# Seven-product MLP pairs: two of the three passes joined into one 512-column product, and the first blocks' weights split by ScalarE and VectorE

## The chip, the cores and the metric

The kernel is one program on one core of a Trainium2 chip. The metric is the device time of one execution in microseconds (us). Before the change the median of three runs is 2317.03 us (2315.73 to 2317.9).

## The reference, cut to what matters

The program runs three transformer-like layers in fp32 on one sequence of T = 512 tokens with D = 1024 features: an RWKV layer, a forgetting-attention layer and a hybrid layer. Each ends in the same kind of MLP, and the change touches these three MLPs alone:

```
def sq_relu_mlp(h, w_in, w_out):
    return jnp.square(jax.nn.relu(h @ w_in)) @ w_out     # h: 512 x 1024, w_in: 1024 x 4096, w_out: 4096 x 1024
# x = x + sq_relu_mlp(rmsnorm(x, gain), w_in, w_out)
```

## The kernel before

**Three passes.** Every fp32 product W x is made from fp32r parts: W is split into whi (rounded) and wlo (the rest), x into hi and lo, and TensorE adds whi*hi + whi*lo + wlo*hi into one PSUM bank. `three` (L732 to L734) does so with 512 columns (tokens) for each of the three. Tokens lie along the columns, features along the 128 partitions.

**Weights.** They come as a stream of blocks of 128 x 1024 (512 KB). SyncE loads block b into `raw[b % 4]`, once block b - 4 is split. As a rule GpSimd makes `whi` (L508, or L582 in the MLP loops; counter `hi_ready`) and then `wlo` (L521; counter `split_ready`), each into slot b % 2, which is free when TensorE has finished block b - 2 (counter `blk`). TensorE waits on `split_ready` ahead of every block.

**An MLP** (`mlp(m, ...)` on TensorE, ScalarE and VectorE, m = 0, 1, 2) has 64 blocks. Blocks 0 to 7 of it are eight tiles of `h @ w_in` made in the plain way (`up`), blocks 8 to 11 are the first part of `@ w_out` (`down`, banks 4 to 7), and then a loop of three turns runs twice per turn: two *pairs* of up tiles (`pair_up`), then four blocks of `down`. The hidden tiles that a `down` reads are those of one group earlier. Blocks 60 to 63 are the last `down`.

**A pair** makes two up tiles (256 rows of the product) from two blocks of weights with seven products instead of eight, by a Strassen-Winograd scheme. Weights are combined into seven forms of 512 columns: VectorE makes four sums `SW` (`form_sum`, L2526), ScalarE rounds each form to `FH` (`form_high`, L1853), GpSimd makes the rest `FL` (`form_lows`, L569). The input is combined once for an MLP into seven forms p = 0 to 6 of 256 columns: `BF` the sum, `BH` its rounded part (ScalarE, L1840), `BL` the rest (VectorE, `x_form_low`, L2512). TensorE runs product p over four k with three passes of 256 columns each (L1184 to L1186), into banks 0, 1, 2, 3 and again 0, 2, 3. Counters: `prod` after p = 0 to 4, `blk` after p = 5 and 6.

**Out of the banks.** For a pair: ScalarE copies bank 0 after p = 0 to `tmpB` (`snapshot`, L1860); VectorE makes V = bank 1 - tmpB (`difference`, L2535), VT = bank 2 + V (L2542), a quarter of the result from bank 3 and VT (`fourth_quarter`, L2550), and later the second (L2555) and third quarter (L2560); ScalarE makes the first (L1865). Relu, square and rounding follow on ScalarE, and the low parts `hidL` on VectorE (`hidden_low`, L2566). The counters `chain` (VectorE) and `snap` (ScalarE) tell TensorE when a bank may be written again.

**Order.** All engines run hand-written orders, each in order. In a half turn VectorE (`group_of_pairs`) does: sums 0 and 1 for the second pair, difference, VT, fourth quarter of the first pair, sums 2 and 3 for the second pair, second and third quarter, then the difference of the second pair, `hidden_low`, VT, `hidden_low`, fourth quarter and the rest. GpSimd does the seven `FL` of the first pair, the seven of the second, and then whi and wlo of the four `down` blocks (`mlp_splits`). Form p = 1 of a pair needs sum 2.

**The start of an MLP.** VectorE takes the eight plain up tiles out of PSUM with relu and scale (L2595), makes their `hidL` (L2607), the scaled input `XR` (8 of L2487), the five sums `BF` (L2497 to L2505) and the seven `BL` (`squares`, then the lines behind it). `add(base + 8, tiles=[0])` (L2615) takes block 8 out of banks 4 and 5; TensorE's block 10 writes these banks again and waits for it, block 11 for the next add.

## Time and profile before

| what | us |
|---|---|
| median of the runs shown | 2317.03 |
| the profiled execution, its own time | 2315.55 |
| its span, first to last instruction | 2313.8 |
| TensorE busy | 2252.0 (97%) |
| VectorE, GpSimd, ScalarE busy | 1439.8, 1363.7, 786.5 |

The profiled execution lies 1.5 us under the median, and 1.75 us of it are outside its span. TensorE's busy time is a union of overlapping instructions, so it is read by the starts of matmuls, not by their durations. The MLPs' pairs and `down` blocks begin at 553, 1182 and 2035 us of the span; a half turn (two pairs, four blocks) takes 41.9 us and there are six in each MLP.

### The profile page before, as it was taken

The page shows a single profiled execution, that of the slowest core. Times are in us where ns is not written, and L with a number is a line of the kernel's source. Part 1 is how long each engine was busy: PE and PEld are TensorE (multiplying, and loading weights), DVE is VectorE, ACT ScalarE, POOL GpSimd, SP SyncE. Part 2 cuts the span into 40 slices and gives each one's busy share as a digit, 9 for nine tenths or more (in the row PEclk, how much of TensorE's full clock was granted, in tenths as well). Part 3 has the DMA queues.
Part 4 walks back from the last instruction along what each step waited for, and adds up shares of the span by engine and source line. Part 5 has one row for each costly group of instructions (what it writes and reads, how often), then busy time and mean ns, then how long its engine had stood idle before and what let it go on. Part 6 is the DMA issues. An engine that isn't in the chain of part 4 may idle for free.

```text
span 2313.8 us, 46712 instructions
## 1 busy us (share of the span) xinstructions
PE 2252.0 (97%) x18202; PEld 1879.7 (81%) x18202; DVE 1439.8 (62%) x1809; ACT 786.5 (34%) x1600; POOL 1363.7 (59%) x918
## 2 busy tenths in 40 slices
PE   8999998998999999999999999999999999899999
PEld 5876888687899877677889988888877778789897
DVE  8797333887655463896876564474057667865553
ACT  5553433323333232353333332111025532233331
POOL 4111001267887765675778877666545456678785
PEclk9999999999999999999999999999999999999999
DMA  4220000222323322111322333223321113223332
GB/s 152 91 92 29 3 4 21 91 91 86 98 91 109 100 93 90 55 38 49 98 83 95 105 101 100 99 92 136 100 73 46 38 46 99 93 74 109 100 100 91
DMA packets 50458, 188.45 MB, mean 81 GB/s; under 512 B 5616, under 2 KB 5744, under 8 KB 49808
## 3 DMA queue, kind: packets, MB, share of 16 engines
q1 hardware_dynamic: 49824, 183.37, 24.3%
q10 hardware_dynamic: 496, 3.12, 0.4%
q8 instruction: 102, 1.67, 0.3%
q14 instruction: 36, 0.29, 0.0%
HBM read 184.30 MB, written 2.10 MB: 81 GB/s over the span
## 4 chain that ended last, share of the span: by engine, by line
PE 86%; DVE 9%; issue 3%; POOL 1%; ACT 1%; DMA 0%; DVEq 0%; POOLq 0%; SPq 0%; ACTq 0%
PE ps L732 18%; PE ps L734 17%; PE ps L733 17%; PE ps L1186 5%; PE ps L1185 5%; PE ps L1184 5%; PE ps L1361 2%; PE ps L1376 2%; PE ps L940 2%; DVE hidL L2607 1%; PE ps L950 1%; DVE XR L2487 1%; PE ps L1342 1%; PE ps L1343 1%; PE ps L745 1%
## 5 line engine op out<-in xcount | busy, mean ns | idle before, releaser
L521 POOL TENSOR_TENSOR wlo<-raw,whi 128x1024 fp32r<-128x1024 f32 (+1 forms) x251 | 598.7, 2385 | 38.8 <-DVE wlo L2664 20.3
L508 POOL TENSOR_SCALAR whi<-raw 128x1024 fp32r<-128x1024 f32 x186 | 215.1, 1156 | 415.4 <-PE ps L734 395.2
L732 PE MATMUL ps<-hidH,whi 128*128 128x512 f32 x768 | 302.2, 394 | 18.3 <-DVE X L2615 17.7
L733 PE MATMUL ps<-hidL,whi 128*128 128x512 f32 x768 | 301.4, 392 | 0.0
L734 PE MATMUL ps<-hidH,wlo 128*128 128x512 f32 x768 | 301.0, 392 | 0.0
L732 PE MATMUL ps<-HH,whi 128*128 128x512 f32 x736 | 298.4, 405 | 0.8 <-POOL wlo L521 0.7
L734 PE MATMUL ps<-HH,wlo 128*128 128x512 f32 x736 | 287.8, 391 | 0.0
L733 PE MATMUL ps<-HL,whi 128*128 128x512 f32 x736 | 287.3, 390 | 0.0
L1184 PE MATMUL ps<-BH,FH 128*128 128x256 f32 x1008 | 285.3, 283 | 0.0
L1185 PE MATMUL ps<-BL,FH 128*128 128x256 f32 x1008 | 285.3, 283 | 0.0
L1186 PE MATMUL ps<-BH,FL 128*128 128x256 f32 x1008 | 285.2, 283 | 0.0
L569 POOL TENSOR_TENSOR FL<-SW,FH 128x512 fp32r<-128x512 f32 x144 | 204.2, 1419 | 78.0 <-ACT FH L1853 78.0
L2615 DVE TENSOR_TENSOR X<-X,ps 128x512 f32<-128x512 f32 x192 | 123.1, 682 | 198.3 <-PE ps L734 198.3
L1853 ACT ACTIVATE FH<-SW 128x512 fp32r<-128x512 f32 x144 | 90.0, 625 | 328.1 <-DVE SW L2526 328.1
L1184 PEld LDWEIGHTS ps<-BH,FH 128*128 128x128 f32 x1008 | 193.4, 192 | 0.9 <-ACT relT L1865 0.2
L1185 PEld LDWEIGHTS ps<-BL,FH 128*128 128x128 f32 x1008 | 193.4, 192 | 0.7
L1186 PEld LDWEIGHTS ps<-BH,FL 128*128 128x128 f32 x1008 | 193.4, 192 | 0.0
L732 PEld LDWEIGHTS ps<-hidH,whi 128*128 128x128 f32 x768 | 145.8, 190 | 49.7 <-issue 19.9
L734 PEld LDWEIGHTS ps<-hidH,wlo 128*128 128x128 f32 x768 | 145.6, 190 | 31.0
L732 PEld LDWEIGHTS ps<-HH,whi 128*128 128x128 f32 x736 | 138.6, 188 | 39.4 <-issue 10.3
L733 PEld LDWEIGHTS ps<-hidL,whi 128*128 128x128 f32 x768 | 145.8, 190 | 29.7
L734 PEld LDWEIGHTS ps<-HH,wlo 128*128 128x128 f32 x736 | 138.4, 188 | 29.7
(527 smaller groups left out, 4720.8 us busy)
## 6 DMA issues: line engine op xcount, KB each, us to landing
raw<-stream SPq DMA_DIRECT2D x336, 512.0 KB, 3.3
X<-xT SPq DMA_DIRECT2D x2, 1024.0 KB, 7.1
X<-xT SPq DMA_DIRECT2D x1, 2048.0 KB, 8.8
CW<-cmpw ACTq DMA_DIRECT2D x1, 2048.0 KB, 9.1
out<-X SPq DMA_DIRECT2D x4, 512.0 KB, 2.7
cst<-consts SPq DMA_DIRECT2D x1, 483.5 KB, 9.6
c2f<-consts ACTq DMA_DIRECT2D x1, 466.0 KB, 3.2
c2s<-consts ACTq DMA_DIRECT2D x1, 466.0 KB, 4.7
```

The source lines that it names most:

```text
L508: pool.tensor_scalar(hi, raw[:, j, :].rearrange("p (k m) -> p k m", k=DT), 1.0, 0.0, ALU.mult, ALU.add)\
L521: return pool.tensor_tensor(wlo[:, s, a:z, :], raw[:, j, a * P:z * P].rearrange("p (k m) -> p k m", k=z - a), whi[:, s, a:z, :].bitcast(F3 ...
L569: low = pool.tensor_tensor(FL[:, p, :, :], form_source(m, r, p), FH[:, p, :, :].bitcast(F32), ALU.subtract)
L732: pe.matmul(acc, whi[:, s, k, :], hi, start=start, stop=False)
L733: pe.matmul(acc, whi[:, s, k, :], lo, start=False, stop=False)
L734: return pe.matmul(acc, wlo[:, s, k, :], hi, start=False, stop=stop)
L940: mm = pe.matmul(square(hp, 1 - c, hp, p), mN[half(c), hp, p, :], mT[half(c), hp, p, :], start=True, stop=True)
L1184: pe.matmul(acc, FH[:, p, k, :], BH[p][:, k, :], start=start and k == 0, stop=False, skip_group_check=True)
L1185: pe.matmul(acc, FH[:, p, k, :], BL[p][:, k, :], start=False, stop=False, skip_group_check=True)
L1186: mm = pe.matmul(acc, FL[:, p, k, :], BH[p][:, k, :], start=False, stop=k == 3, skip_group_check=True)
L1853: act.activation(FH[:, p, :, :], form_source(m, r, p), ACT.Copy).then_inc(count("form_hi", 0)[0], 1)
L2615: ins = dve.tensor_tensor(X[:, e, :], X[:, e, :], ps[:, 4 + 2 * (j % 2) + o, :], ALU.add)
```

## The change

`BH[p]` and `BL[p]` are laid beside each other for each k, so that one matmul with FH reads both, 512 columns, into a whole bank, and the third pass (FL with BH) adds 256 columns to the bank's second half. The result of a product is then the bank's first half plus its second half. The reads of the banks become 512 wide, three of them are followed by an add of two halves (`halves`), and the first quarter becomes a ScalarE copy and a VectorE add. In the start of an MLP, blocks 4 to 11 are split by ScalarE (`weight_high`) and VectorE (`weight_low`) in a new hand-written order, and the low parts of the input forms 4, 5 and 6 move from VectorE to GpSimd. Lines with only "..." stand for what is left out.

```diff
-    BH = [at(f"BH{p}", [P, 4, TH], form_at[p], F32R) for p in range(7)]
-    BL = [at(f"BL{p}", [P, 4, TH], form_at[p] + 4096, F32R) for p in range(7)]
-    BF = [at(f"BF{p}", [P, 4, TH], form_at[p] + 4096) for p in range(7)]
+    BX = [at(f"BX{p}", [P, 4, 2, TH], form_at[p], F32R) for p in range(7)]
+    BZ = [at(f"BZ{p}", [P, 4, 2, TH], form_at[p]) for p in range(7)]
+    BH, BL, BF = [b[:, :, 0, :] for b in BX], [b[:, :, 1, :] for b in BX], [b[:, :, 1, :] for b in BZ]
...
+                for p in (4, 5, 6):
+                    pool.wait_ge(*count("x_form_hi", 7 * m + p + 1))
+                    pool.tensor_tensor(BL[p], BF[p], BH[p].bitcast(F32), ALU.subtract).then_inc(count("x_form_lo_p", 0)[0], 1)
...
-            splits(y0 + 6, START["mlp0"] + 12)
+            splits(y0 + 6, START["mlp0"] + 4)
...
-                            pe.wait_ge(*count("x_form_lo", 7 * m + p + 1))
+                            pe.wait_ge(*(count("x_form_lo", 4 * m + p + 1) if p < 4 else count("x_form_lo_p", 3 * m + p - 3)))
...
-                        pe.wait_ge(*[count("snap", 2 * Q), count("chain", 5 * Q - 4), count("chain", 5 * Q - 1), count("chain", 5 * Q),
-                                     count("snap", 2 * Q + 1), count("chain", 5 * Q + 2), count("chain", 5 * Q + 3)][p])
-                        acc = ps[:, bank, 0:TH]
+                        pe.wait_ge(*[count("chain", 9 * Q - 4), count("chain", 9 * Q - 8), count("chain", 9 * Q - 3), count("chain", 9 * Q - 1),
+                                     count("snap", 2 * Q + 1), count("chain", 9 * Q + 2), count("chain", 9 * Q + 3)][p])
                         for k in range(4):
-                            pe.matmul(acc, FH[:, p, k, :], BH[p][:, k, :], start=start and k == 0, stop=False, skip_group_check=True)
-                            pe.matmul(acc, FH[:, p, k, :], BL[p][:, k, :], start=False, stop=False, skip_group_check=True)
-                            mm = pe.matmul(acc, FL[:, p, k, :], BH[p][:, k, :], start=False, stop=k == 3, skip_group_check=True)
+                            pe.matmul(ps[:, bank, :], FH[:, p, k, :], BX[p][:, k, :, :].rearrange("p a t -> p (a t)"), start=start and k == 0,
+                                      stop=False, skip_group_check=True)
+                            mm = pe.matmul(ps[:, bank, TH:T], FL[:, p, k, :], BH[p][:, k, :], start=False, stop=k == 3, skip_group_check=True)
                         mm.then_inc(count("prod", 0)[0] if p < 5 else S("blk"), 1)
...
+                def weight_high(o):
+
+                    b = base + o
+                    act.wait_ge(S("split_ready"), b)
+                    act.wait_ge(S("blk"), b - (SPL - 1))
+                    act.wait_ge(S(f"raw_in{b % RAW}"), (b // RAW + 1) * 16)
+                    act.activation(whi[:, b % SPL, :, :], raw[:, b % RAW, :].rearrange("p (k m) -> p k m", k=DT), ACT.Copy).then_inc(S("hi_ready"), 1)
...
+                def second_group():
+
+                    weight_high(6)
+                    squared(1, 0)
+                    weight_high(7)
+                    squared(1, 1)
+                    square_high(1, 0)
+                    x_form_high(0)
+                    x_form_high(1)
+                    weight_high(8)
+                    squared(1, 2)
+                    square_high(1, 1)
+                    x_form_high(2)
+                    x_form_high(3)
+                    weight_high(9)
+                    squared(1, 3)
+                    square_high(1, 2)
+                    x_form_high(4)
+                    square_high(1, 3)
+                    x_form_high(5)
+                    x_form_high(6)
+                    weight_high(10)
+                    weight_high(11)
...
-                    act.wait_ge(*count("chain", 5 * Q - 4))
-                    act.activation(tmpB[:, 0:TH], ps[:, 0, 0:TH], ACT.Copy).then_inc(count("snap", 0)[0], 1)
-
-                def first_quarter(i, r):
+                    act.wait_ge(*count("chain", 9 * Q - 8))
+                    act.activation(tmpB[:, :], ps[:, 0, :], ACT.Copy).then_inc(count("snap", 0)[0], 1)
+
+                def first_half(i, r):
 
                     act.wait_ge(*count("prod", 5 * pair_number(m, i, r) + 5))
-                    act.activation(zT[r % 2][0][:, 0:TH], ps[:, 0, 0:TH], ACT.Relu).then_inc(count("snap", 0)[0], 1)
-
...
+                def positive(i, r, o):
+
+                    z = zT[r % 2][o]
...
-                V, VT, M2 = tmpA[:, 0:TH], tmpA[:, TH:T], tmpB[:, 0:TH]
+                V, W, M2 = tmpA[:, :], ssq[:, :], tmpB[:, :]
+
+                def halves(out, of):
+
...
-                    dve.tensor_tensor(V, ps[:, 1, 0:TH], M2, ALU.subtract).then_inc(count("chain", 0)[0], 1)
+                    dve.wait_ge(*count("chain", 9 * Q))
+                    dve.tensor_tensor(V, ps[:, 1, :], M2, ALU.subtract).then_inc(count("chain", 0)[0], 1)
...
-                    dve.tensor_tensor(VT, ps[:, 2, 0:TH], V, ALU.add).then_inc(count("chain", 0)[0], 1)
+                    dve.wait_ge(*count("chain", 9 * Q + 1))
+                    dve.tensor_tensor(W, ps[:, 2, :], V, ALU.add).then_inc(count("chain", 0)[0], 1)
...
+                    dve.tensor_tensor(W, ps[:, 3, :], W, ALU.subtract).then_inc(count("chain", 0)[0], 1)
                     dve.wait_ge(S("full"), FT * m + 4 * (2 * i + 2 + r // 2))
-                    dve.tensor_tensor(zT[r % 2][1][:, TH:T], ps[:, 3, 0:TH], VT, ALU.subtract).then_inc(count("chain", 0)[0], 1)
+                    dve.wait_ge(*count("chain", 9 * Q + 3))
+                    halves(zT[r % 2][1][:, TH:T], W).then_inc(count("chain", 0)[0], 1)
+
+                def first_quarter(i, r):
+
+                    z = zT[r % 2][0][:, 0:TH]
+                    dve.wait_ge(*count("snap", 2 * pair_number(m, i, r) + 2))
+                    dve.tensor_tensor(z, ps[:, 0, TH:T], z, ALU.add).then_inc(count("chain", 0)[0], 1)
 
                 def second_quarter(i, r):
 
+                    Q = pair_number(m, i, r)
                     dve.wait_ge(S("blk"), pair_block(m, i, r) + 1)
-                    dve.tensor_tensor(zT[r % 2][0][:, TH:T], ps[:, 2, 0:TH], V, ALU.add).then_inc(count("chain", 0)[0], 1)
+                    dve.wait_ge(*count("chain", 9 * Q + 4))
+                    dve.tensor_tensor(W, ps[:, 2, :], V, ALU.add).then_inc(count("chain", 0)[0], 1)
+                    dve.wait_ge(*count("chain", 9 * Q + 6))
+                    halves(zT[r % 2][0][:, TH:T], W).then_inc(count("chain", 0)[0], 1)
 
                 def third_quarter(i, r):
 
+                    Q = pair_number(m, i, r)
                     dve.wait_ge(S("blk"), pair_block(m, i, r) + 2)
-                    dve.tensor_tensor(zT[r % 2][1][:, 0:TH], V, ps[:, 3, 0:TH], ALU.subtract).then_inc(count("chain", 0)[0], 1)
+                    dve.wait_ge(*count("chain", 9 * Q + 7))
+                    dve.tensor_tensor(V, V, ps[:, 3, :], ALU.subtract).then_inc(count("chain", 0)[0], 1)
+                    dve.wait_ge(*count("chain", 9 * Q + 8))
+                    halves(zT[r % 2][1][:, 0:TH], V).then_inc(count("chain", 0)[0], 1)
...
+                    first_quarter(i, r)
...
+                def weight_low(o):
+
+                    b = base + o
+                    dve.wait_ge(S("hi_ready"), b + 1)
+                    dve.tensor_tensor(wlo[:, b % SPL, :, :], raw[:, b % RAW, :].rearrange("p (k m) -> p k m", k=DT), whi[:, b % SPL, :, :].bitcast(F32),
+                                      ALU.subtract).then_inc(S("split_ready"), 1)
...
+                def second_group():
+
+                    read(1, 0)
+                    weight_low(6)
+                    x_scaled(6)
+                    x_scaled(7)
+                    x_sum(1)
+                    read(1, 1)
+                    weight_low(7)
+                    x_sum(4)
+                    square_low(1, 0)
+                    x_sum(2)
+                    read(1, 2)
+                    weight_low(8)
+                    x_form_low(0)
+                    square_low(1, 1)
+                    x_sum(5)
+                    read(1, 3)
+                    weight_low(9)
+                    x_sum(6)
+                    square_low(1, 2)
+                    x_form_low(1)
...
                 add(base + 8, tiles=[0])
+                weight_low(10)
                 x_form_low(2)
                 x_form_low(3)
                 add(base + 8, tiles=[1])
-                x_form_low(4)
-                x_form_low(5)
-                x_form_low(6)
+                weight_low(11)
                 with dve.Fori(0, 3) as i:
...
```

The other moves follow from these: `first_group` on both engines puts blocks 4 and 5 among the first four tiles in the same manner, the counters of a pair on VectorE go from five to nine, `fourth_quarter`'s first instruction keeps its wait for p = 3, and GpSimd's splits end at block 3 (also for the second and third MLP).

## Rows read from the trace of the kernel before

**Rows 1.** Page, part 1: TensorE's busy time and instructions.

```profile
PE 2252.0 (97%) x18202; PEld 1879.7 (81%) x18202; DVE 1439.8 (62%) x1809; ACT 786.5 (34%) x1600; POOL 1363.7 (59%) x918
```

**Rows 2.** Stretches: length; busy us (instructions) of PE, PEld, DVE, ACT, POOL; clock, DMA.

```profile
595.09:615.24 20.15, 20.15 (x170) 20.15 (x168) 10.94 (x17) 8.50 (x18) 18.41 (x14) 1.00 0.33 105
615.24:637.02 21.78, 21.78 (x98) 18.02 (x97) 13.39 (x13) 6.59 (x12) 15.91 (x10) 1.00 0.30 97
```

**Rows 3.** Groups by line and shape: busy us, mean ns of one.

```profile
L521 POOL TENSOR_TENSOR wlo<-raw,whi 128x1024 fp32r<-128x1024 f32 x215 | 549.9, 2558 | 38.1 <-DVE wlo L2664 20.3
...
L1184 PE MATMUL ps<-BH,FH 128*128 128x256 f32 x1008 | 285.3, 283 | 0.0
...
L2615 DVE TENSOR_TENSOR X<-X,ps 128x512 f32<-128x512 f32 x192 | 123.1, 682 | 198.3 <-PE ps L734 198.3
...
L2271 DVE TENSOR_TENSOR wlo<-raw,whi 128x1024 fp32r<-128x1024 f32 x24 | 30.2, 1258 | 6.1 <-POOL whi L508 5.6
...
L1840 ACT ACTIVATE BH<-BF 128x1024 fp32r<-128x1024 f32 x15 | 15.9, 1057 | 14.3 <-DVE BF L2505 9.6 <-DVE BF L2497 2.0 <-DVE BF L2503 1.6
```

**Rows 4.** TensorE in order of time (start, us): first matmuls of the stretches of rows 2.

```profile
595.09 0.28 PE L1184 MATMUL ps<-BH,FH 128*128 128x256 f32 x1
...
615.24 0.40 PE L732 MATMUL ps<-hidH,whi 128*128 128x512 f32 x1
```

**Rows 5.** GpSimd in order of time, the same stretch.

```profile
602.98 1.29 POOL L569 TENSOR_TENSOR FL<-SW,FH 128x512 fp32r<-128x512 f32 x1 [1.65 <-ACT FH L1853]
...
609.27 1.74 POOL L569 TENSOR_TENSOR FL<-raw,FH 128x512 fp32r<-128x512 f32 x1
610.99 1.49 POOL L582 TENSOR_SCALAR whi<-raw 128x1024 fp32r<-128x1024 f32 x1
612.56 2.41 POOL L521 TENSOR_TENSOR wlo<-raw,whi 128x1024 fp32r<-128x1024 f32 x1
```

**Rows 6.** VectorE in order of time, the same stretch.

```profile
601.13 0.42 DVE L2550 TENSOR_TENSOR relT<-ps,tmpA 128x256 f32<-128x256 f32 x1 [1.02 <-PE ps L1186]
601.48 1.41 DVE L2526 TENSOR_TENSOR SW<-SW,raw 128x512 f32<-128x512 f32 x2
...
608.34 0.42 DVE L2535 TENSOR_TENSOR tmpA<-ps,tmpB 128x256 f32<-128x256 f32 x1 [2.56 <-PE ps L1186]
608.68 1.18 DVE L2566 TENSOR_TENSOR hidL<-sqrT,hidH 128x512 fp32r<-128x512 f32 x1
...
611.49 0.41 DVE L2550 TENSOR_TENSOR relB<-ps,tmpA 128x256 f32<-128x256 f32 x1
```

**Rows 7.** ScalarE in order of time, the same stretch.

```profile
602.27 0.63 ACT L1853 ACTIVATE FH<-SW 128x512 fp32r<-128x512 f32 x1 [4.30 <-DVE SW L2526]
...
607.02 0.36 ACT L1860 ACTIVATE tmpB<-ps 128x256 f32<-128x256 f32 x1
```

**Rows 8.** Waits of TensorE: us in total, times, longest.

```profile
PE ps L732 <- DVE X L2615: 17.7, 3, 6.8
```

**Rows 9.** TensorE in order of time: block 10 of the first and second MLP.

```profile
539.48 0.76 PE L732 MATMUL ps<-hidH,whi 128*128 128x512 f32 x1 [6.85 <-DVE X L2615]
...
1169.71 0.67 PE L732 MATMUL ps<-hidH,whi 128*128 128x512 f32 x1 [4.00 <-DVE X L2615]
```

**Rows 10.** VectorE and GpSimd in order of time, start of the first MLP.

```profile
495.74 3.73 DVE L2487 SCALAR_TENSOR_TENSOR XR<-X,vec,rstd 128x512 f32<-128x512 f32 x2
...
538.06 1.27 DVE L2615 TENSOR_TENSOR X<-X,ps 128x512 f32<-128x512 f32 x2
...
496.22 2.71 POOL L521 TENSOR_TENSOR wlo<-raw,whi 128x1024 fp32r<-128x1024 f32 x1
```

**Rows 11.** Stretches, columns as in rows 2: behind the waits for block 8's add.

```profile
540.00:544.00 4.00, 4.00 (x11) 3.09 (x10) 4.00 (x6) 0.00 (x0) 0.00 (x0) 0.50 0.00 0
544.00:548.00 4.00, 4.00 (x17) 3.20 (x16) 4.00 (x5) 0.63 (x1) 0.37 (x1) 0.85 0.00 0
548.00:552.00 4.00, 4.00 (x19) 3.31 (x18) 2.88 (x4) 3.33 (x6) 4.00 (x3) 1.00 0.01 2
```

More of the change, by code:

```diff
@@ L2494, in x_sum @@
                         dve.wait_ge(*count("x_scaled", DT * m + DT))
-                    out = BF[p][:, :, :]
+                    out = BF[p]
                     if p == 1:
@@ L2526, in form_sum @@
                     dve.tensor_tensor(SW[:, r % 2, n, :], first, second, ALU.add).then_inc(count("form_sum", 0)[0], 1)
-                V, VT, M2 = tmpA[:, 0:TH], tmpA[:, TH:T], tmpB[:, 0:TH]
+                V, W, M2 = tmpA[:, :], ssq[:, :], tmpB[:, :]
+                def halves(out, of):
+                    return dve.tensor_tensor(out, of[:, 0:TH], of[:, TH:T], ALU.add)
                 def difference(i, r):
@@ L2584, in group_of_pairs @@
                     fourth_quarter(i, n)
+                    first_quarter(i, n)
                     second_quarter(i, n)
                     third_quarter(i, n)
[L2588 to L2608 removed]
@@ new lines, in square_low, with first_group @@
+                def square_low(g, j):
+                    dve.wait_ge(S("hidhi"), FT * m + g * 4 + j + 1)
+                    dve.tensor_tensor(hidL[g][:, j, :], sqrT[:, j % 2, :], hidH[g][:, j, :].bitcast(F32), ALU.subtract).then_inc(S("hid"), 1)
+                def first_group():
+                    read(0, 0)
+                    read(0, 1)
+                    weight_low(4)
+                    read(0, 2)
+                    square_low(0, 0)
+                    x_scaled(0)
+                    x_scaled(1)
+                    square_low(0, 1)
+                    read(0, 3)
+                    weight_low(5)
+                    x_scaled(2)
+                    x_scaled(3)
+                    square_low(0, 2)
+                    x_scaled(4)
+                    x_scaled(5)
+                    square_low(0, 3)
```

115 lines of the change are left out of this document (45 added, 70 removed).

## The prediction

> **What bounds the kernel now.** I read the page first. TensorE is busy for 2252.0 of 2313.8 us [rows 1], so outside of a few waits only work taken off TensorE, or a wait of TensorE, can move the time. The groups by shape say which work the change takes off: 3 x 1008 matmuls of 256 columns, 36 pairs of 84 [rows 3]. The stretches by time give their real pace: two pairs are 168 matmuls in 20.15 us, 119.9 ns each, and the four down blocks behind them 96 matmuls of 512 columns in 21.78 us, 226.9 ns each [rows 2]. Half the columns take more than half the time: 106.7 ns at 2.4 GHz and 13 more for 256, 213.3 and 14 more for 512. Something like 13.3 ns belongs to each matmul, not to its columns.
>
> Then I asked how close the other engines run behind TensorE, and this view decides the case. GpSimd is busy for 18.41 of the 20.15 us of two pairs [rows 2]. Behind its last FL it makes whi and wlo of the first down block, and that wlo ends at 612.56 + 2.41 = 614.97; TensorE takes up this block at 615.24 [rows 4, 5]. The reader is to see a margin of 0.27 us in 20. There are 18 places of this kind: in sixteen the margin is 0.25 to 0.27, and in the first half turn of the second and third MLP it is used up already. So the pairs are bound by two engines at once: TensorE at 20.15, GpSimd's row of FLs plus one block at about 19.9 and a small step of semaphores.
>
> Last, the waits: TensorE waits 17.7 us in three places for VectorE's add of block 8, one in each MLP, 6.85, 4.00 and 6.85 us [rows 8, 9].
>
> **Part 1, the joined pass on TensorE.** A k step goes from three matmuls of 256 (360 ns) to one of 512 and one of 256 (227 + 120 = 347). Two pairs have 56 k steps: 56 x 0.0133 = 0.75 us less, in 18 half turns 13.4 us. This is the whole gain that the joined pass can give. If the 256 that is left ran at 107, the pairs would be another 0.7 us shorter, which by what follows would become waiting. The Trainium skill, "TensorE: Matmul & The Clock Gate", section "Wait - 56ns, not 53.3ns?", gives N / 2.4 GHz + about 2.5 ns for a matmul; by this the joining would save 56 x 2.5 = 0.14 us in two pairs. The rows' own 13.3 ns differs, and is what I use.
>
> **Part 2, GpSimd's row of work gets no shorter and starts later.** All times here are counted from the first matmul of two pairs (595.09). GpSimd's first FL is for the first pair; its FL for p = 1 of the second starts at 602.98 - 595.09 = 7.89, released by ScalarE's FH (start 7.18), which waits for VectorE's sum 2, which starts behind the fourth quarter at 6.39 [rows 5 to 7]. The fourth quarter starts at 6.04, which is 0.28 behind product 4's end (4 x 1.44 = 5.76). New: product 4 ends at 4 x 1.387 = 5.55, the fourth quarter starts at 5.83, its read is 512 wide, and the add of the halves waits for it. For a 512-wide instruction behind which one waits I take 0.72, the step between the two sums (1.41 for the two, less the second one's own 0.68 to 0.69) [rows 6]. An add of 256 columns with both inputs in SBUF isn't in the trace; it lies between nothing and a 512-wide one (0.68), and the 256-wide read of PSUM (0.42, of which 0.35 before the next starts) is the nearest [rows 6]. So sum 2 starts at 5.83 + 0.72 + 0.35 = 6.90, 0.51 later, and the FL at 8.40. From this FL's start to the end of wlo it is 614.97 - 602.98 = 11.99 [rows 5]. TensorE can't take the block before 8.40 + 11.99 + 0.13 = 20.5 (0.13 is the step that I read where TensorE did wait here). Before it was 20.15. The 0.75 us of TensorE are lost to GpSimd, and 0.37 on top: this is the floor.
>
> **Part 3, three more adds that take turns with GpSimd.** An instruction of VectorE with two SBUF inputs and one of GpSimd don't overlap in this trace: two XR take 3.73, because GpSimd's wlo of 2.71 stands between them [rows 10]; `hidL` takes 1.18 where an unhindered 512-wide one takes 0.68, and the last FL 1.74 instead of 1.29 [rows 5, 6]. Reads of PSUM aren't hindered (0.68 on average over 192) [rows 3]. The Trainium skill, "SBUF - State Buffer", says that VectorE and GpSimd hold a shared pair of ports one instruction at a time and the loser waits for all of it; this speaks against the change's three `halves` and moved low parts, and the trace agrees. A pair gets three `halves`. Two or three of them fall into the FLs between 8.4 and 20, and each holds GpSimd up by 0.34: 0.7 to 1.0.
>
> The same turns make VectorE late. I walked the three engines through the half turn with the durations above. The first quarter's add comes behind sum 3 and ScalarE's copy, ends at 9.97, and product 0 of the second pair (due 9.71) starts at 10.07: 0.36 waited. Second quarter 9.9, its halves behind an FL until 11.2, third quarter and halves behind another until 12.8; ScalarE's relu and square follow, and only then the snapshot, now 512 wide, until 14.5 (it ended at 607.38 - 595.09 = 12.3 before [rows 7]). Then difference, `hidL` behind the last FL until 17.2, and the second pair's bank 2 read until 17.8 where TensorE wants bank 2 at 17.0: 0.86 waited. The next `hidL` and the fourth read free bank 3 at 19.5: 0.35. Then wlo: 0.33. Sum 1.90, so two pairs take 20.15 - 0.75 + 1.90 = 21.3. The same walk for the kernel before comes out 0.15 above its rows, so I take 21.15: 1.0 us more in each of 18 half turns, **+18.0**. The floor of part 2 is +0.37, the end without that correction and with one more turn lost +1.5. In the first half turn of an MLP the FLs are later; the walk has 0.7 more there, of which before already lost 1.2 in the second and third MLP: **+0.9**.
>
> **Part 4, the start of an MLP.** Before, VectorE comes to the add of block 8 at 538.06 [rows 10], though TensorE began its wait for it, with block 9 behind it, at 539.48 - 6.85 = 532.6 [rows 9], and block 8 was done a block (24 x 0.227 = 5.44) earlier, at 527.2. VectorE is freed of its waits for the wlo of eight blocks (2.4 each when alone [rows 5]) and of three BL; it takes over eight `weight_low` at 1.26 (1.2 when nothing is in the way) and ScalarE eight of 1.06 [rows 3]. With GpSimd quiet, VectorE keeps up with TensorE's 5.44 us for a block through block 7: each `weight_low` ends about 3 us ahead of its need. The end is different. Block 7 ends at 521.5 to 521.7. ScalarE makes block 9's whi until 522.6, square and round until 523.8, form 4 until 524.8; only then can GpSimd begin its three BL of about 2.4 each (a tensor_tensor of the same shape as wlo). VectorE has four instructions with two SBUF inputs behind block 9's wlo, and meets all three BL: sum 6 until 525.05; BL 4 to 527.4; `hidL` 528.0; BL 5 to 530.4; form 1's low 531.6; BL 6 to 534.0; `hidL` 534.6; add of block 8 to 535.8; and then block 10's wlo, which is now VectorE's own, to 537.0. TensorE is at block 10 at 532.5, so it waits some 4.6 with the semaphore. This replaces 6.85, 4.00 and 6.85 [rows 9]: 17.7 - 13.8 = **-3.9**. If GpSimd's three turns cost nothing the wait is gone, -17.7.
>
> The granted clock was 0.50 behind the first such wait and 0.85 in the next 4 us: 11 and 17 matmuls where 19 run at full clock, 10 x 0.227 = 2.3 us [rows 11]. Behind the second MLP's wait of 4.00 the clock fell too: 8 matmuls in 3.29 busy us where 14 fit, 1.5 and a little after it, 1.7 in all; behind the third's 8 in 3.43 and a little after, 2.0. Waits of 4.6 should cost about 1.7 each: 6.0 - 5.1 = **-0.9**.
>
> SyncE's loads still follow `split_ready`, of which each block's comes within a us or two of where it came, and a slot is asked for four blocks (21.8 us) before its block is used, so the loads cost nothing; were this cover gone, ScalarE's whi would show waits for the load.
>
> **Sum.** +18.0 + 0.9 - 3.9 - 0.9 = +14.1 us. The profiled execution would go from 2315.55 to about 2329.7, and its span from 2313.8 to 2327.9. The median lies 1.5 above the execution: 2317.0 + 14.1 = 2331.1, rounded 2331.
>
> **Rivals.**
> (a) *VectorE and GpSimd keep up in the pairs and TensorE's gain arrives.* 18 x -0.75 = -13.4, with the start -18.3: 2299. For it: VectorE is busy only 10.94 of 20.15 us [rows 2]. Against it: the 0.27 us of margin, which can let at most that much through; -0.75 needs GpSimd to finish 0.5 earlier, and nothing is taken from it.
> (b) *Faster by the start alone.* If GpSimd's three BL find their place between VectorE's waits, VectorE has done block 10's wlo at 529.8, ahead of 532.5 (TensorE's own time there), and the waits (17.7) and the slow clock (6.0) are gone: -23.7. With the pairs near their floor, 18 x 0.37 = +6.7, this is 2300. It decides where block 10's wlo ends before 532.5, and for the sign the pairs must lose under 1.3 us per half turn. For it: the early part of the start is clean. Against it: form 4's BH isn't there before 524.8, and 7.2 us of BL meet 6 us of VectorE's work in 7.7 us.
> (c) *It cancels*, pairs at +0.37 to 0.6 and the start at -4.8 to -8: 2315 to 2322, that is inside what a measurement can tell, 0.2% or 4.6 us.
> (d) *The turns are worse than walked:* every `halves` waits for a whole FL, the chain slips by 0.8 more in a half turn: +28, 2345.
>
> **Chances.** My forecast, slower by 6 to 25 us (2323 to 2342): 0.58. (d): 0.13. (c): 0.12. (b) or part of it, with the pairs slower but the start winning: 0.12. (a): 0.05. From these: slower by over 0.2% 0.71 (the forecast and (d)), within 0.2% 0.13 ((c) and a little of (b)), faster 0.16 ((a) and most of (b)). The range leaves out about 0.09 below and 0.08 above: 2306 to 2344; the likeliest case's own range is 2323 to 2342.
>
> **What the changed kernel's profile would show.** Matmuls with FH at 512 columns start 0.347 apart in couples (part 1). FL for p = 1 of the second pair starts about 8.4 behind the first matmul (part 2). TensorE has new short waits in the pairs, for VectorE's reads into ssq and for GpSimd's wlo, and two pairs take 21.1 instead of 20.15 (part 3). Block 10 waits about 4.6 us for VectorE's wlo, with three BL of GpSimd in front of it (part 4). The prediction is wrong if two pairs take under 20.5, which would mean that GpSimd's row isn't what I say, or if block 10 doesn't wait.

## The result and the profile after

The changed kernel takes 2323.76 us (13 runs), the kernel before 2317.9 beside it (13 runs): ratio 1.0024, interval 1.0015 to 1.0033. It is slower by about 5.9 us, as I said, but by less than half of the 14.1 that I forecast. The profiled execution took 2320.85 us with a span of 2319.1, against 2315.55 and 2313.8: 5.3 more.

Page, part 1, after (answers to [rows 1]):

```profile
PE 2257.1 (97%) x17194; PEld 1822.9 (79%) x17194; DVE 1569.3 (68%) x1968; ACT 825.3 (36%) x1624; POOL 1298.7 (56%) x879
```

1008 matmuls are gone and TensorE's busy time is not less. VectorE has 130 us more and GpSimd 65 less, but where it counts, in the pairs, GpSimd is as full as before. The stretches, after (answers to [rows 2]):

```profile
592.07:612.88 20.81, 20.51 (x113) 17.02 (x112) 16.07 (x21) 8.81 (x17) 18.47 (x14) 1.00 0.32 102
612.88:634.75 21.87, 21.87 (x96) 18.12 (x97) 16.95 (x18) 7.22 (x13) 16.40 (x10) 1.00 0.30 97
```

Two pairs went from 20.15 to 20.81, the down blocks behind them from 21.78 to 21.87. The reader is to see 113 matmuls where there were 170, in more time. Counted from start to start, fifteen of the 18 half turns went from 41.94 to 42.7.

Where the time goes is read best from the first matmul of each MLP's pairs. In the kernel before these stand at 553.14, 1182.32 and 2035.44. TensorE in order of time, after:

```profile
547.32 0.39 PE L1186 MATMUL ps<-BX,FH 128*128 128x512 f32 x1
...
1182.98 0.39 PE L1186 MATMUL ps<-BX,FH 128*128 128x512 f32 x1
...
2036.54 0.39 PE L1186 MATMUL ps<-BX,FH 128*128 128x512 f32 x1
```

The change stands at -5.82, then +0.66, +1.10 and, at the end, +5.3. So the first start wins 5.8, the first MLP's pairs lose 6.5 (and the second start wins nothing); the second MLP's pairs lose 3.5 and the third start wins 3.1; the third MLP's pairs lose 4.2. In sum the pairs lose 14.2. The starts win 8.9, of which 2.0 were already there at 374 us of the span, ahead of anything that the change touches.

TensorE's waits, after (answers to [rows 8]):

```profile
PE ps L735 <- DVE wlo L2640: 11.9, 3, 4.0
...
PE ps L1186 <- DVE relT L2588: 3.7, 18, 0.2
...
PE ps L1186 <- DVE ssq L2572: 1.6, 4, 1.1
...
PE ps L1186 <- DVE ssq L2579: 1.1, 1, 1.1
```

Block 10 waits three times 4.0 us, now for VectorE's wlo. Its wait for block 8's add (17.7) is gone. The new waits in the pairs are small, 18 times 0.2 for the first quarter's add (L2588), which frees bank 0 for the second pair's product 0. Two are not small: 1.1 us for `ssq`, L2572 (bank 2), and 1.1 for L2579 (bank 3). Both are in the first half turn of the first MLP (read below, with experiment 7).

**The start, as walked.** VectorE and GpSimd in order of time, start of the first MLP, after (answers to [rows 10]):

```profile
523.27 2.90 DVE L2653 TENSOR_TENSOR hidL<-sqrT,hidH 128x512 fp32r<-128x512 f32 x1
526.09 3.42 DVE L2537 TENSOR_TENSOR BX<-BZ,BX 128x1024 fp32r<-128x1024 f32 x1
529.43 2.85 DVE L2653 TENSOR_TENSOR hidL<-sqrT,hidH 128x512 fp32r<-128x512 f32 x1
532.21 1.27 DVE L2703 TENSOR_TENSOR X<-X,ps 128x512 f32<-128x512 f32 x2
533.40 1.21 DVE L2640 TENSOR_TENSOR wlo<-raw,whi 128x1024 fp32r<-128x1024 f32 x1
```

```profile
523.03 8.71 POOL L591 TENSOR_TENSOR BX<-BZ,BX 128x1024 fp32r<-128x1024 f32 x3 [33.02 <-ACT BX L1883]
```

Three BL in 8.71 us with a 512-wide `hidL`, form 1's low and another `hidL` between them: `hidL` takes 2.90 and 2.85 where 0.68 is its own length. Block 8's add and block 10's wlo follow, and the wlo ends at 534.61. TensorE, the same stretch (answers to [rows 9]):

```profile
534.67 0.50 PE L735 MATMUL ps<-hidH,whi 128*128 128x512 f32 x1 [3.98 <-DVE wlo L2640]
```

**Inside two pairs, as walked.** GpSimd in order of time, after (answers to [rows 5]):

```profile
600.58 1.29 POOL L569 TENSOR_TENSOR FL<-SW,FH 128x512 fp32r<-128x512 f32 x1 [2.26 <-ACT FH L1896]
...
603.05 1.50 POOL L569 TENSOR_TENSOR FL<-SW,FH 128x512 fp32r<-128x512 f32 x1
604.52 1.47 POOL L569 TENSOR_TENSOR FL<-raw,FH 128x512 fp32r<-128x512 f32 x1
...
608.46 1.49 POOL L582 TENSOR_SCALAR whi<-raw 128x1024 fp32r<-128x1024 f32 x1
610.04 2.71 POOL L521 TENSOR_TENSOR wlo<-raw,whi 128x1024 fp32r<-128x1024 f32 x1
```

FL for p = 1 starts 600.58 - 592.07 = 8.51 behind the first matmul (8.40 forecast, 7.89 before), and wlo ends at 20.68; TensorE takes up the block 0.13 later. From the start of the one to the end of the other are 12.17 us, where it was 11.99. VectorE (answers to [rows 6]):

```profile
598.73 0.42 DVE L2557 TENSOR_TENSOR relT<-ssq 128x256 f32<-128x256 f32 x1
599.07 1.41 DVE L2551 TENSOR_TENSOR SW<-SW,raw 128x512 f32<-128x512 f32 x2
...
609.57 0.92 DVE L2612 TENSOR_TENSOR hidL<-sqrT,hidH 128x512 fp32r<-128x512 f32 x1
610.42 0.68 DVE L2579 TENSOR_TENSOR ssq<-ps,ssq 128x512 f32<-128x512 f32 x1
611.13 1.91 DVE L2557 TENSOR_TENSOR relB<-ssq 128x256 f32<-128x256 f32 x1
```

The 256-wide `halves` takes 0.42 alone and 1.91 behind a wlo. Sum 2 starts at 7.00 (6.90 forecast). TensorE, the second pair's product 0:

```profile
602.32 0.50 PE L1186 MATMUL ps<-BX,FH 128*128 128x512 f32 x1 [0.20 <-DVE relT L2588]
602.65 0.28 PE L1188 MATMUL ps<-BX,FL 128*128 128x256 f32 x1
```

It starts 0.48 behind the matmul ahead of it, where 0.12 is the pace: 0.36 waited, as forecast. Then 0.33 pass to its second matmul where 0.23 is the pace; a restart costs 0.1 more.

### The profile page after: what moved, and what is told of

It reads as the page before. It is cut to its first block, busy times and chain, and to the rows that moved or that the text cites. A ratio compares the mean times of both kernels' runs of the same rounds, so it can differ in the third digit from the quotient of the medians.

```text
span 2319.1 us, 45032 instructions
## 1 busy us (share of the span) xinstructions
PE 2257.1 (97%) x17194; PEld 1822.9 (79%) x17194; DVE 1569.3 (68%) x1968; ACT 825.3 (36%) x1624; POOL 1298.7 (56%) x879
## 4 chain that ended last, share of the span: by engine, by line
PE 83%; DVE 8%; issue 4%; ACT 3%; POOL 1%; DMA 0%; ACTq 0%; DVEq 0%; SPq 0%; POOLq 0%
PE ps L735 19%; PE ps L736 18%; PE ps L737 18%; PE ps L1186 7%; PE ps L1188 3%; PE ps L1363 2%; PE ps L1378 2%; PE ps L943 2%; PE ps L953 1%; PE ps L1344 1%; PE ps L1345 1%; PE ps L748 1%; ACT FH L1896 1%; DVE hidL L2653 1%; POOL wlo L521 1%
## 5 line engine op out<-in xcount | busy, mean ns | idle before, releaser
L521 POOL TENSOR_TENSOR wlo<-raw,whi 128x1024 fp32r<-128x1024 f32 (+1 forms) x227 | 540.4, 2380 | 36.8 <-DVE wlo L2750 20.3
L508 POOL TENSOR_SCALAR whi<-raw 128x1024 fp32r<-128x1024 f32 x162 | 182.5, 1127 | 382.1 <-PE ps L737 358.7
L1186 PE MATMUL ps<-BX,FH 128*128 128x512 f32 x1008 | 362.3, 402 | 7.2 <-DVE relT L2588 3.7
L735 PE MATMUL ps<-hidH,whi 128*128 128x512 f32 x768 | 302.9, 394 | 13.1 <-DVE wlo L2640 11.9
L1188 PE MATMUL ps<-BX,FL 128*128 128x256 f32 x1008 | 282.6, 280 | 0.0
L1186 PEld LDWEIGHTS ps<-BX,FH 128*128 128x128 f32 x1008 | 189.3, 188 | 64.6 <-DVE relT L2588 9.4
L1188 PEld LDWEIGHTS ps<-BX,FL 128*128 128x128 f32 x1008 | 190.3, 189 | 0.7
L736 PEld LDWEIGHTS ps<-HL,whi 128*128 128x128 f32 x736 | 138.8, 189 | 26.4 <-issue 1.2
L569 POOL TENSOR_TENSOR FL<-raw,FH 128x512 fp32r<-128x512 f32 x108 | 151.2, 1400 | 0.0
```

The lines of the kernel that those rows point to most:

```text
L508: pool.tensor_scalar(hi, raw[:, j, :].rearrange("p (k m) -> p k m", k=DT), 1.0, 0.0, ALU.mult, ALU.add)\
L521: return pool.tensor_tensor(wlo[:, s, a:z, :], raw[:, j, a * P:z * P].rearrange("p (k m) -> p k m", k=z - a), whi[:, s, a:z, :].bitcast(F3 ...
L569: low = pool.tensor_tensor(FL[:, p, :, :], form_source(m, r, p), FH[:, p, :, :].bitcast(F32), ALU.subtract)
L735: pe.matmul(acc, whi[:, s, k, :], hi, start=start, stop=False)
L736: pe.matmul(acc, whi[:, s, k, :], lo, start=False, stop=False)
L1186: pe.matmul(ps[:, bank, :], FH[:, p, k, :], BX[p][:, k, :, :].rearrange("p a t -> p (a t)"), start=start and k == 0, stop=False, skip_grou ...
```

## The experiments

Each ratio is to the kernel before, in runs beside it on the same chip. "Half turn" is from first matmul of two pairs to the next one's.

**1 and 2. The two parts alone.** `start_only` has the change's start (ScalarE's and VectorE's split, GpSimd's three BL) and the old pairs; `pairs_only` has the joined pairs and the old start.

```diff
 # start_only, against before (with first_group/second_group on ScalarE and VectorE)
+                for p in (4, 5, 6):
+                    pool.wait_ge(*count("x_form_hi", 7 * m + p + 1))
+                    pool.tensor_tensor(BL[p][:, :, :], BF[p][:, :, :], ...)
-            splits(y0 + 6, START["mlp0"] + 12)
+            splits(y0 + 6, START["mlp0"] + 4)
 # pairs_only, against after: the same lines the other way round
```

> The kernel before with the change's start of an MLP alone (blocks 4 to 11 split by ScalarE and VectorE, low parts of forms 4 to 6 on GpSimd), pairs as they were. My theory (the change's loss is in the pairs, its start gains): block 10's three waits go from 6.85, 4.00, 6.85 us to about 4.1 each, the granted clock still falls once behind each, two pairs take 20.15 us again; 7 to 8 us faster than before, about 2310 (ratio 0.997). Rival (the start's gain belongs to the pairs' new layout or is chance of the clock): within 2 us of before.

> The kernel before with the change's pairs alone, start of an MLP as it was. My theory: two pairs take 20.8 us and half a turn 42.7 in place of 41.9, 14 us in 18 half turns, a little more in the first half turns: 13 to 16 us slower than before, about 2332 (ratio 1.006). Rival (start and pairs aren't independent, because a start that ends earlier moves the first half turns): under 10 us slower.

Measured: `start_only` 2306.76 us, ratio 0.996 (0.9944 to 0.9975); `pairs_only` 2329.4, ratio 1.0058 (1.0044 to 1.0072). The stretches of two pairs, first of `start_only`, then of `pairs_only`:

```profile
589.37:609.52 20.15, 20.15 (x169) 20.14 (x168) 10.97 (x17) 8.51 (x18) 18.43 (x14) 1.00 0.34 105
```

```profile
591.90:612.72 20.82, 20.48 (x114) 17.02 (x112) 16.09 (x21) 8.82 (x17) 18.48 (x14) 1.00 0.32 102
```

The signs are as forecast: the start wins (10.7 us of the medians, 10.0 of the profiled executions, more than the 7 to 8 that I expected), the pairs lose (12.0 and 13.5). In `start_only` all first half turns take 20.15 for their two pairs; in the kernel before those of the second and third MLP took 21.13 and 20.41. `start_only` still waits 12.0 us at its three blocks 10, so this wait belongs to the new start, not to the pairs. The two ratios add up to -0.4 + 0.58 = +0.18%, 4.2 us, and both together give 5.9; the difference lies inside the intervals. The traces do show one place where the parts don't add up, worth 2.1 us: the first MLP's first two pairs take 20.15 in `start_only`, 20.81 in `pairs_only`, and 22.93 in the change. What happens there is read below, with experiment 7.

**3 and 4. GpSimd's three low parts given back to VectorE.** Nothing else changes: in `start_lows_on_vector` on `start_only`, in `change_lows_on_vector` on the change.

```diff
-                for p in (4, 5, 6):   # GpSimd
-                    pool.wait_ge(*count("x_form_hi", 7 * m + p + 1))
-                    pool.tensor_tensor(BL[p], ...)
                 weight_low(11)        # VectorE
+                x_form_low(4)
+                x_form_low(5)
+                x_form_low(6)
```

> As the start-only kernel, but the low parts of forms 4 to 6 stay on VectorE, behind its last weight split. My theory (GpSimd's three low parts take turns with VectorE right in front of block 10's split, and nothing else makes this wait): VectorE is done with block 10's wlo near 529 to 530, ahead of TensorE's 532; the three waits are gone, the granted clock doesn't fall behind them, at most 1 us is given back in the first pairs: about 20 us faster than before, 2296 to 2300 (ratio 0.991 to 0.993). Rival (VectorE is short of time there whoever makes the low parts; the wait moves to the first products, which need sums and low parts later by 3.6 us): 2 to 4 us per MLP waited at the first pair, 2303 to 2310.

> The changed kernel with the low parts of forms 4 to 6 on VectorE, behind its last weight split. My theory: the same 12 to 14 us less than the changed kernel that the start-only pair of kernels shows, with the pairs at 20.8 us: about 2311, 6 us or so faster than before (ratio 0.997). Rival as for the start-only kernel: the wait moves to the first pair, whose VectorE is already late; 2316 to 2322.

Measured: 2292.82, ratio 0.9896 (0.9881 to 0.9911), and 2308.59, ratio 0.9962 (0.9947 to 0.9977). So the three low parts cost 14 to 15 us of the medians in either kernel (11 to 12 between the profiled executions): block 10 no longer waits and the clock doesn't fall behind it. `start_lows_on_vector` is 24.6 us faster than before, where I expected about 20. VectorE in `change_lows_on_vector`:

```profile
524.35 0.69 DVE L2650 TENSOR_TENSOR hidL<-sqrT,hidH 128x512 fp32r<-128x512 f32 x1
524.95 1.22 DVE L2534 TENSOR_TENSOR BX<-BZ,BX 128x1024 fp32r<-128x1024 f32 x1
526.09 0.68 DVE L2650 TENSOR_TENSOR hidL<-sqrT,hidH 128x512 fp32r<-128x512 f32 x1
526.69 1.28 DVE L2700 TENSOR_TENSOR X<-X,ps 128x512 f32<-128x512 f32 x2
527.88 1.22 DVE L2637 TENSOR_TENSOR wlo<-raw,whi 128x1024 fp32r<-128x1024 f32 x1
...
534.15 3.49 DVE L2534 TENSOR_TENSOR BX<-BZ,BX 128x1024 fp32r<-128x1024 f32 x3
```

The same instructions that took 2.90, 3.42 and 2.85 take 0.69, 1.22 and 0.68, and block 10's wlo ends at 529.1 instead of 534.6. All three BL take VectorE 3.49 us; on GpSimd they took 8.71 and lengthened VectorE's three instructions between them by 6.6. The price is paid once per MLP, two pairs of 21.18 (old pairs) or 22.05 (joined) in the first half turn, because sums and FLs come later.

**5 and 6. What does the joining give TensorE if nothing else changes?** `joined_matmuls_old_reads` is the kernel before with the joined matmuls and `BX`; the reads stay 256 wide, and there are no `halves`, so the products' low parts are left out of the result. `joined_old_reads_whi_scalar` moves in addition the whi of the first down block of each half turn from GpSimd to ScalarE.

```diff
-                            pe.matmul(acc, FH[:, p, k, :], BH[p][:, k, :], ...)
-                            pe.matmul(acc, FH[:, p, k, :], BL[p][:, k, :], ...)
-                            mm = pe.matmul(acc, FL[:, p, k, :], BH[p][:, k, :], ...)
+                            pe.matmul(ps[:, bank, :], FH[:, p, k, :], BX[p][:, k, :, :]..., ...)
+                            mm = pe.matmul(ps[:, bank, TH:T], FL[:, p, k, :], BH[p][:, k, :], ...)
 # the second kernel, in addition:
+                    if j:
                         pool.tensor_scalar(whi[:, slot % SPL, :, :], ...)
+                    down_high(i, r)      # ScalarE, behind hidden_high(i, r, 1): the same whi for j = 0
```

> The kernel before with the joined matmuls alone: 512 columns for FH, 256 for FL, but the banks are read as before, 256 wide and with no adds of halves (so the low parts of the products, which lie in the second halves of the banks, are left out of the result). It tells TensorE's own saving from what VectorE and ScalarE do for it. Theory 1 (GpSimd's row of work is the floor): TensorE would need 19.77 us for two pairs (0.353 a couple, as the changed kernel's first pair shows), wlo of the first down block still ends 19.8 to 19.9 behind the pairs' start, two pairs take 19.9 to 20.0; 3 to 4 us faster in all. Theory 2 (no floor, VectorE's reads alone cost the change its gain): 19.77, 7 us faster. Theory 3 (joined couples cost as much as three of 256): 20.15, no change.

> As the kernel with joined matmuls and old reads (low parts left out of the result), and whi of the first down block of every half turn on ScalarE instead of GpSimd, 1.1 us off GpSimd's row. Theory 1 (GpSimd's row is the floor): two pairs fall to TensorE's own 19.77, 7 us faster than before in all, 3 to 4 faster than without this. Theory 2 and 3: no difference to the kernel without it.

Measured: 2314.75, ratio 0.9995 (0.9985 to 1.0005), and 2308.28, ratio 0.997 (0.9958 to 0.9982). Two pairs, first the one, then the other:

```profile
592.43:612.29 19.86, 19.86 (x113) 17.04 (x112) 11.05 (x17) 8.50 (x18) 18.24 (x14) 1.00 0.34 106
```

```profile
593.29:613.06 19.77, 19.77 (x113) 17.16 (x112) 11.07 (x17) 9.45 (x19) 18.16 (x14) 1.00 0.33 107
```

In the first, GpSimd's wlo ends at 19.73 and TensorE goes on at 19.86: the floor of part 2. Most of its two pairs take 19.9, and behind the wait the down blocks take 21.90 instead of 21.79. So a half turn falls only from 41.94 to 41.8, which is 2.5 us in 18; I expected 3 to 4, and the ratio's interval reaches from 3.5 us faster to 1.2 slower. With the whi off GpSimd's row TensorE gets its own 19.77 (half turn 41.59), and that is 56 x 0.353, not 56 x 0.347. So the joining is worth 0.38 us in two pairs, half of the 0.75 in my sum. Of these 0.38 GpSimd lets about 0.25 through even without any `halves`, and 0.1 of that is lost again behind the wait.

**7. The same relief for the change.** I expected the whi's move to win here too.

```diff
 # change_whi_scalar, against after: the edit of experiment 6
+                    if j:
                         pool.tensor_scalar(whi[:, slot % SPL, :, :], ...)
+                    down_high(i, r)
```

> The changed kernel with whi of the first down block of every half turn on ScalarE, behind its hidden_high, 1.1 us off GpSimd's row. Theory 1 (in the changed kernel the last wait, 0.33 us, is for GpSimd's wlo, the 0.36 and 0.22 before it are for VectorE's reads): two pairs go from 20.82 to about 20.5, 5 to 6 us faster than the changed kernel. Rival (VectorE's chain is as late as GpSimd, so it only changes what is waited for): under 2 us.

Measured: 2346.05, ratio 1.0131 (1.0115 to 1.0147). This theory fell: half turns take 44.0 instead of 42.7. GpSimd and VectorE of this kernel:

```profile
606.51 2.38 POOL L521 TENSOR_TENSOR wlo<-raw,whi 128x1024 fp32r<-128x1024 f32 x1 [0.70 <-ACT whi L1936]
```

```profile
606.28 0.68 DVE L2582 TENSOR_TENSOR ssq<-ps,tmpA 128x512 f32<-128x512 f32 x1
606.88 2.56 DVE L2622 TENSOR_TENSOR hidL<-sqrT,hidH 128x512 fp32r<-128x512 f32 x1
609.36 0.68 DVE L2589 TENSOR_TENSOR ssq<-ps,ssq 128x512 f32<-128x512 f32 x1
```

and TensorE's waits in this half turn:

```profile
PE ps L1187 <- DVE ssq L2589: 1.4, 1, 1.4
```

wlo, freed of the whi, starts 0.37 us ahead of VectorE's second `hidL`, which then takes 2.56 us instead of 0.92. Behind it stands the read that frees bank 3, and TensorE's product 6 waits 1.4 for it. In the change the same `hidL` starts 0.47 us ahead of wlo (609.57 and 610.04, above). Which of two instructions comes first decides over 1.4 us. In the change's first half turn of the first MLP the order turns at two places. GpSimd and VectorE there, after:

```profile
558.33 1.27 POOL L569 TENSOR_TENSOR FL<-SW,FH 128x512 fp32r<-128x512 f32 x1
...
564.84 2.69 POOL L521 TENSOR_TENSOR wlo<-raw,whi 128x1024 fp32r<-128x1024 f32 x1
```

```profile
558.35 1.54 DVE L2557 TENSOR_TENSOR relT<-ssq 128x256 f32<-128x256 f32 x1
...
565.82 2.26 DVE L2612 TENSOR_TENSOR hidL<-sqrT,hidH 128x512 fp32r<-128x512 f32 x1
```

The second quarter's `halves` comes 0.02 behind an FL and takes 1.54; in the half turn read above it starts at 602.89, 0.16 ahead of the FL, and takes 0.51. (The read before it starts 0.2 later here; why, I did not find.) VectorE's chain is then 1.0 us late, which makes the wait for bank 2. So wlo is there before the second `hidL`, which takes 2.26, and this makes the wait for bank 3. The two pairs take 22.93.

**8. Is it the alternation of widths?** `change_passes_grouped` issues four matmuls of 512 and then four of 256 for each product.

```diff
                         for k in range(4):
                             pe.matmul(ps[:, bank, :], FH[:, p, k, :], BX[p]..., ...)
+                        for k in range(4):
                             mm = pe.matmul(ps[:, bank, TH:T], FL[:, p, k, :], BH[p][:, k, :], ...)
```

> The changed kernel with the order of the matmuls of a product changed: four of 512 columns, then four of 256, instead of four couples. In the changed kernel a couple takes 0.353 us where a run of 512 takes 0.227 and a run of 256 0.120 apiece, 0.347 together. If the 6 ns are paid at each change of width or of weights behind a short matmul, a product takes 1.39 us instead of 1.41 and two pairs lose up to 0.3 us of TensorE's time, hidden in part by the other engines: 0 to 4 us faster than the changed kernel. If they are paid per 512-column matmul of this kind (its operand or its weights), nothing changes.

Measured: 2320.68, ratio 1.0029 (1.002 to 1.0039), half turn 42.68. A product takes 1.40 instead of 1.41, and nothing of it reaches the time (two pairs 20.79 for 20.81). TensorE in order of time:

```profile
589.60 1.07 PE L1186 MATMUL ps<-BX,FH 128*128 128x512 f32 x4
590.51 0.64 PE L1189 MATMUL ps<-BX,FL 128*128 128x256 f32 x4
```

**9 and 10. The fourth quarter's `halves` behind sums 2 and 3.** By part 2 this add stands in front of sum 2, and so of GpSimd's whole row. `change_halves_later` moves it behind the two sums; `change_lows_vector_halves_later` does so in `change_lows_on_vector`.

```diff
                     form_sum(i, n, 3)
+                    fourth_halves(i, r)      # taken out of fourth_quarter(i, r)
                     first_quarter(i, r)
```

> The changed kernel with one instruction moved in VectorE's order: the add of the fourth quarter's halves goes behind form sums 2 and 3 of the next pair. My theory (this add stands in front of sum 2 and so in front of ScalarE's FH and GpSimd's whole row of FLs; it costs 0.35 to 0.4 us twice, once for GpSimd's row and once for the first quarter's add that product 0 of the second pair waits for): sum 2 starts at 6.6 instead of 7.0 behind the pairs' first matmul, the FL for p = 1 at 8.15 instead of 8.50, the 0.36 us wait of the second pair is gone, two pairs take 20.4 to 20.5 instead of 20.82; 6 to 8 us less than the changed kernel, about level with the kernel before to 2 us faster. Rival (the reads that are 512 wide and the turns with GpSimd set the time, not this place): under 2 us less.

> Both mends of the change in one: low parts of forms 4 to 6 on VectorE, and the fourth quarter's halves behind sums 2 and 3. If both theories hold and add up, 6 to 8 us less than the first mend alone (which stood at 0.9962 of before): ratio about 0.993, and still above the kernel that has the new start with the old pairs and low parts on VectorE (0.9896), since two pairs stay above 20.15 us.

Measured: 2317.63, ratio 0.9992 (0.9982 to 1.0003), and 2304.38, ratio 0.9935 (0.9917 to 0.9952). VectorE and the stretch of the first:

```profile
596.52 1.41 DVE L2551 TENSOR_TENSOR SW<-SW,raw 128x512 f32<-128x512 f32 x2
597.85 0.42 DVE L2557 TENSOR_TENSOR relT<-ssq 128x256 f32<-128x256 f32 x1
```

```profile
589.98:610.45 20.47, 20.24 (x114) 17.05 (x112) 16.11 (x21) 8.82 (x17) 18.59 (x14) 1.00 0.33 104
```

Sum 2 starts at 6.54 instead of 7.00, FL for p = 1 at 8.04, wlo ends at 20.34 and two pairs take 20.47: one instruction of 0.42 us moved by two places gives 0.34 us in each half turn. It also takes away product 0's wait, and it brings the first MLP's first half turn from 22.93 to 20.50. With it the change is level with the kernel before, and no more: two pairs of 20.47 are still over 20.15.

**11. The best of all this.** `start_lows_vector_whi_scalar` is `start_lows_on_vector` with experiment 6's whi on ScalarE: old pairs, 256 wide.

> The fastest kernel so far (new start, low parts on VectorE, old pairs) with whi of the first down block of a half turn on ScalarE. In fifteen of eighteen half turns TensorE is the bound and nothing changes; in the first of each MLP, 21.18 us now, GpSimd's row is 1 us late, and this falls to 20.2 to 20.5: 2 to 3 us less, ratio 0.988 to 0.989. Rival (as it went with the changed kernel: GpSimd's wlo, now earlier, stands before VectorE's second hidL, and bank 3 comes late): 0 to 5 us more.

Measured: 2292.67, ratio 0.9885 (0.9864 to 0.9906). The two pairs of the first half turn and of the next:

```profile
547.07:567.56 20.49, 20.41 (x169) 20.20 (x168) 13.38 (x17) 10.53 (x21) 20.49 (x14) 1.00 0.31 101
589.35:609.50 20.15, 20.15 (x169) 20.14 (x168) 10.97 (x17) 9.44 (x19) 18.44 (x14) 1.00 0.35 108
```

The first half turn's 21.18 became 20.49; 3 x 0.7 = 2 us are too few for the times to tell it from 0.9896. The best kernels are these two: the change's start without GpSimd's low parts, and without the joined product.

## Why the prediction was right or wrong

**What bounds the kernel** held. Two pairs stand between TensorE's row and GpSimd's, 0.27 us apart. Experiments 5 and 6 show the floor directly: 19.86 with GpSimd's row as it was, 19.77 without the whi in it.

**Part 1** was right in kind and twice too large. A couple of 512 and 256 takes 0.353 us (19.77 / 56), where I summed rows of runs of one width to 0.347. The joining gives 0.38 in two pairs, not 0.75. By the Trainium skill, "TensorE: Matmul & The Clock Gate", section "Wait - 56ns, not 53.3ns?", which gives N / 2.4 GHz + 2.5 ns for a matmul, an estimate would be 0.14; no stretch here bears that out, and the measured 0.38 decides. Grouping the widths gives back 0.01 a product, under 0.2 in fourteen (experiment 8), so the alternation explains a part at most. Nor is 0.353 fixed: by the starts of matmuls, products 1 to 3 of the second pair take 1.39 each, which is 0.347 a couple, in 3 of the change's 18 half turns and in 11 of the 18 of `change_halves_later`. What decides between the two stays open.

**Part 2** held: sum 2 at 7.00 (6.90), FL at 8.51 (8.40), shown as the cause by experiment 9.

**Part 3 is the step that failed, by size.** The sum had 1.90 us of waits in two pairs; the trace has 1.04. Term by term: product 0 waits 0.36 as forecast, and 0.1 for its restart; product 5 waits 0.22 and 0.1 where I had 0.86; product 6 doesn't wait where I had 0.35; wlo is awaited 0.25 where I had 0.33. The last engine to be ready is GpSimd: 8.51 + 12.17 + 0.13 = 20.81, the time of two pairs. So the term that I had wrong is its holding up by the turns: I said 0.7 to 1.0, and measured are 12.17 - 11.99 = 0.2. Two of the three `halves` delay an FL, by 0.2 each (1.50 and 1.47 instead of 1.29) and not by 0.34; the third comes behind the start of wlo. And my sum only added turns. The two `hidL` had theirs already: before, they lengthened the last FL (1.74 for 1.29) and the whi; now they meet the whi (1.49 as before) and wlo (2.71 for 2.41), and the last FL is free.

VectorE is also less late in the end. My walk holds up to the snapshot, which ends at 14.56 (14.5). Behind it the second `hidL` gets in ahead of wlo and takes 0.92, and bank 3 is free in time. Product 5's wait is short for another reason too: TensorE, with its slower couples and a restart, comes there at 17.4 and not at 17.0. So the gain that part 1 had too large is met by a wait that part 3 had too large, and neither reaches the time. So 19.77 + 1.04 = 20.81 instead of 20.15 - 0.75 + 1.90 = 21.3, from which I took 0.15 off: +0.67 for two pairs, not +1.0, with 0.1 more in the down blocks behind them. In 18 half turns that is +13.9 for my +18.0.

That VectorE comes first at these meetings is a matter of 0.16 us at one place and 0.47 at another, and neither my walk nor its rivals named it as a threshold. Where the order turns, 1 us or more is lost at once (experiment 7; the first MLP's first half turn, at two places). The Trainium skill, "SBUF - State Buffer", section "SBUF: two separate sides", says that the one of the two that starts first has the shared ports for its whole instruction and the other waits for all of it. The trace agrees: `hidL` takes 2.56 behind a wlo of 2.38.

**First half turns:** +0.9 forecast. Against the 0.77 of the others the first MLP's lost 2.0 more, the second's 1.1 less (the kernel before had lost that already), the third's 0.4 less: +0.5. Right in sum, not in place.

**Part 4** held in its order to the instruction, and its times, counted from TensorE's arrival at block 10, are within 0.6 us: wait 3.98 for 4.6. Three times 0.6 is why the waits fell by 17.7 - 11.9 = 5.8 us, not 3.9. The clock gave 1.3, not 0.9. The stretch at half clock behind the first wait:

```profile
535.69:539.11 3.42, 3.42 (x10) 2.64 (x8) 3.42 (x5) 0.02 (x1) 0.00 (x0) 0.50 0.48 153
```

A 512-column matmul starts every 0.43 us there, for 0.23: 8 matmuls, 1.6 us, in each MLP. In the kernel before the first MLP had 5.69 us of TensorE's work at this clock, 2.7 lost. That GpSimd's three BL are the cause of the wait is shown by experiments 3 and 4.

**Not in the sum** is a piece of chance. The kernel before was profiled with another stretch at half clock, ahead of all that the change touches; then the kernel before, and after about the same place:

```profile
371.09:374.50 3.41, 3.41 (x135) 3.41 (x131) 0.50 (x1) 0.60 (x1) 0.00 (x0) 0.50 0.00 0
```

```profile
371.00:374.50 3.50, 3.46 (x155) 3.22 (x145) 0.69 (x1) 2.17 (x4) 0.00 (x0) 1.00 0.16 60
```

The changed kernel stands 2.0 us ahead behind it, of which 1.3 were won within this stretch; the rest is drift between the two executions just ahead of it. Three of the thirteen profiled executions have such a stretch at 366 to 371 us (the kernel before, `start_lows_on_vector`, `start_lows_vector_whi_scalar`), and ten have none, though all of them do the same work up to the first MLP. The medians contain such chances on both sides.

The sum as measured: pairs and first half turns 14.4 for 18.9, start 7.1 for 4.8, chance 2.0 for nothing: +5.3 for +14.1. Of the 8.8 us of error, half is the pairs', which is part 3's size, a quarter the start, a quarter the chance. The medians' 5.9 has a share of chance too, which one profile of each kernel doesn't tell.

**The rivals.** (a) is out: of TensorE's gain no more than about 0.25 us in two pairs can pass GpSimd (experiment 5), and the change's pairs lose. (b), "faster by the start alone", named the right condition: block 10's wlo ahead of TensorE's arrival. The change misses it by 4 us, and `change_lows_on_vector`, which meets it, is 8.8 us faster than before. (c) had a start of -4.8 to -8 where 7.1 were won, and put the pairs' loss at 0.6 at most where it is 0.77. (d) needs the order to turn in every half turn; `change_whi_scalar` is such a kernel, and it came to 2346 where (d) said 2345, though through one `hidL` behind wlo, not through the `halves`. In the change itself only the first MLP's first half turn has a `halves` of this kind.

## What to carry to other kernels

Before shortening the engine that bounds a loop, measure by how much the next engine's row of work is shorter: here 0.27 us in 20, and of a gain of 0.38 about 0.25 came through. Moving work onto an engine that takes turns with the one relieved can cost more than the work (three low parts: 3.5 us on VectorE, 8.7 on GpSimd, 14 to 15 us of the kernel's time in three MLPs). When a new short instruction is added to an in-order queue, put it behind the instruction that gates another engine's row (0.34 us per half turn for moving one add), and look which of two engines that take turns comes first at each meeting: relief for one of them can turn the order and cost more than it gives.

## What was not expected of the hardware

- A 512- and a 256-column matmul in turn cost 0.353 us, where runs of one width give 0.227 + 0.120 = 0.347 [rows 2], but in some half turns the couples run at 0.347 too; behind a wait, the first 512-column matmul holds the next for 0.33 instead of 0.23.
- VectorE's 256-wide fp32 add of two SBUF inputs takes 0.42 us, as long as a 256-wide read of PSUM, and up to 1.91 beside GpSimd's wlo.
- The same three 128x1024 subtractions take 3.49 us on VectorE alone and 8.71 on GpSimd beside VectorE.
